# Second out projection tile for all tokens ahead of the third, and a re-ordered routing stage: weights copied aside, embedding products later, all rows on POOL, strips waited for one by one

## The reference, cut to what matters

```python
y = jax.nn.sigmoid(ma) * ya + jax.nn.sigmoid(mb) * yb
h = layer_norm_2(DEEPNORM_ALPHA * h + y @ w_out[i], ln1_g[i], ln1_b[i])
m = moe(h, w_router[i], b_router[i], w_up[i], b_up[i], w_down[i], b_down[i])
h = layer_norm_2(DEEPNORM_ALPHA * h + m, ln2_g[i], ln2_b[i])
h = h + jax.nn.sigmoid(h @ w_ple_gate[i] + b_ple_gate[i]) * (p[i] @ w_ple[i])
```

## Time and profile before

| | |
|---|---|
| median of 3 runs | 2378.13 us (2377.28 to 2379.11) |
| profiled execution, its own time | 2378.32 us |
| its span, first to last instruction | 2376.5 us |
| mean granted TensorE clock | 0.999 of full speed |
| busy | PE 98%, PEld 68%, DVE 50%, ACT 35%, POOL 8% |
| read from HBM | 663.69 MB, 280 GB/s over the span |

### The profile page before, as it was taken

How to read it: one execution, slowest core, us unless ns; L and a number is a source line. 1 busy time by engine, 2 the same in 40 slices (tenths; PEclk the granted TensorE clock), 3 DMA queues, 4 the chain that set the end, 5 groups by cost and what they waited for, 6 DMA issues and landing times.

```text
span 2376.5 us, 33062 instructions
## 1 busy us (share of the span) xinstructions
PE 2327.8 (98%) x13409; PEld 1604.4 (68%) x13409; DVE 1189.4 (50%) x1621; ACT 835.6 (35%) x1028; POOL 192.8 (8%) x90
## 2 busy tenths in 40 slices
PE   9999999999999999999999999999999999999999
PEld 8889989888888998988899983333333333333335
DVE  5668766756755876675686772112211111111115
ACT  4554344544544434454448341111111111111113
POOL 0002502200200250220020000000000000000000
PEclk9999999999999999999999999999999999999999
DMA  8765454565556545456546689999999999999995
GB/s 271 235 203 175 150 188 146 180 204 180 195 185 206 176 145 192 144 178 203 185 144 197 204 314 407 428 427 428 428 425 429 427 427 427 427 428 428 427 425 229
DMA packets 222323, 666.37 MB, mean 280 GB/s; under 512 B 10099, under 2 KB 164339, under 8 KB 191620
## 3 DMA queue, kind: packets, MB, share of 16 engines
q1 hardware_dynamic: 222212, 664.77, 73.6%
HBM read 663.69 MB, written 1.05 MB: 280 GB/s over the span
## 4 chain that ended last, share of the span: by engine, by line
PE 80%; DMA 15%; SPq 4%; DVE 0%; issue 0%; ACT 0%; ACTq 0%; POOLq 0%; DVEq 0%
PE ps L829 17%; PE ps L790 13%; DMA ring<-in_w_up_dram 13%; PE ps L811 12%; PE ps L1426 9%; PE ps L817 6%; PE ps L1474 6%; PE ps L916 4%; SPq L483 2%; DMA work<-in_w_down_dram 2%; PE ps L1391 1%; PE ps L1400 1%; PE ps L1006 1%; PE ps L1632 1%; PE ps L1266 1%; PE ps L1058 1%
## 5 line engine op out<-in xcount | busy, mean ns | idle before, releaser
L2305 DVE TENSOR_TENSOR ring_halves<-ring,ring_halves 128x2048 fp32r<-128x2048 f32 (+1 forms) x214 | 527.1, 2473 | 190.0 <-ACT ring_halves L1732 189.7
L1732 ACT CAST ring_halves<-ring 128x2048 fp32r<-128x2048 f32 (+1 forms) x214 | 401.4, 1876 | 114.9 <-PE ps L829 90.4
L2886 DVE TENSOR_TENSOR work<-ps,work 128x256 f32<-128x256 f32 x64 | 26.9, 420 | 633.3 <-PE ps L1460 633.3
L811 PE MATMUL ps<-x_halves,ring_halves 128*128 128x512 f32 x1280 | 326.5, 392 | 0.1
L1426 PE MATMUL ps<-ring,work 128*64 128x512 f32 x1248 | 278.1, 595 | 24.0 <-DMA ring<-in_w_up_dram 24.0
L829 PE MATMUL ps<-ring_halves,work_halves 128*128 128x512 f32 x1184 | 288.7, 391 | 0.3
L790 PE MATMUL ps<-x_halves,ring_halves 128*128 128x256 f32 x2208 | 274.7, 285 | 0.1
L790 PEld LDWEIGHTS ps<-x_halves,ring_halves 128*128 128x128 f32 x2208 | 267.6, 192 | 2.1 <-issue 0.7
L811 PEld LDWEIGHTS ps<-x_halves,ring_halves 128*128 128x128 f32 x1280 | 230.2, 189 | 41.5 <-issue 0.5
L829 PEld LDWEIGHTS ps<-ring_halves,work_halves 128*128 128x128 f32 x1184 | 221.4, 188 | 48.7 <-issue 3.1
L1720 ACT COPY hT<-ps 128x512 f32<-128x512 f32 x96 | 56.2, 585 | 497.5 <-PE ps L1426 460.5
(11 more groups left out here) (294 smaller groups left out, 2447.9 us busy)
## 6 DMA issues: line engine op xcount, KB each, us to landing
ring<-in_w_up_dram SPq DMA_DIRECT2D x77, 2048.0 KB, 36.5
work<-in_w_up_dram SPq DMA_DIRECT2D x37, 2048.0 KB, 41.6
ring<-in_w_down_dram SPq DMA_DIRECT2D x36, 2048.0 KB, 40.4
ring<-in_w_in_dram SPq DMA_DIRECT2D x52, 1024.0 KB, 5.2
ring<-in_ffn_up_dram SPq DMA_DIRECT2D x44, 1024.0 KB, 5.4
ring<-in_ffn_down_dram SPq DMA_DIRECT2D x44, 1024.0 KB, 4.9
ring<-in_ffn_gate_dram SPq DMA_DIRECT2D x43, 1024.0 KB, 5.4
work<-in_w_down_dram SPq DMA_DIRECT2D x19, 2048.0 KB, 36.6
```

The source lines that it names most:

```text
L811: return pe.matmul(ps[:, b, :], high[:, o:o + P], x_both[:, :, k, :], start=(k == 0), stop=(k == DT - 1))
L1732: nc.scalar.copy(second_half(high_of(name)[:], name), second_half(ring[:, s, :], name))\
L2305: v.tensor_tensor(second_half(ring_halves[s][:], name), second_half(ring[:, s, :], name), second_half(high_of(name)[:].bitcast(F32), name) ...
```

## The change

1. PE takes tile `w2o1` for both token tiles before `w2o2`. The transposes of t = 0 stand in the middle of the last tile of t = 1, behind its first half.
2. `router(t)` waits strip by strip, in the order 0, 4, 1, 5, 2, 6, 3, 7, where the even places are ACT's and the odd ones DVE's. The logits of t = 1 go to bank 1 (were in bank 2).
3. DVE's `best` is cut into `highest` (up to the cast) and `choose` (the marks). The order is: rows of t = 1, `highest(0)`, strips of t = 1, `choose(0)`, `highest(1)`, `choose(1)`.
4. POOL makes `h` of both token tiles; DVE's two instructions on rows (L2800, L2807) are gone. `h_ready` comes after POOL's fourth instruction.
5. ACT copies `w_ple` (128x2048) into `hn` once `h_ready` is there ("wple kept"). SP's loads into `V` and `IG` wait for that and for the fourth half product of t = 0.
6. The embedding products of t = 0 stand behind `router(1)` and around the counts; those of t = 1 are taken from the copy inside `few()`: one before `gate_up` of expert 0, three between it and the next gather. The gates' transpose moves into the branch too. ACT's copies and DVE's "rows in" move with them, DVE's into `step(HEAD)` after its selection.

```diff
-                    sp.wait_ge(dve_done.sem, dve_done.at("rows"))
-                    sp.wait_ge(pe_full.sem, pe_full.at(("ple", 1, 1)))
+                    sp.wait_ge(act_done.sem, act_done.at("wple kept"))
+                    sp.wait_ge(pe_full.sem, pe_full.at(("ple", 0, 1)))
...
-            for j in (1, 2):
-                y_part(j)
+            y_part(1)
+            for t in range(TT):
                 for kk in range(2):
-                    w2o_part(j, kk, 0)
+                    mm = w2o_part(1, kk, t)
+            release(mm, "w2o1")
+            y_part(2)
+            for kk in range(2):
+                w2o_part(2, kk, 0)
             y_part(3)
             full(w2o_last(0), ("t0", after))
-            for j in (1, 2):
-                for kk in range(2):
-                    mm = w2o_part(j, kk, 1)
-                release(mm, f"w2o{j}")
-            transposes(after, 0, hn)
-            release(w2o_last(1), "w2o3")
+            for kk in range(2):
+                mm = w2o_part(2, kk, 1)
+            release(mm, "w2o2")
+            release(w2o_last(1, lambda: transposes(after, 0, hn)), "w2o3")
...
-                for k in range(DT):
-                    mm = pe.matmul(ps[:, 2 * t, 0:32], hT[:, k, t * P:t * P + P], w(ROUTER + k * 32, 32),
+                for k in (0, 4, 1, 5, 2, 6, 3, 7):
+                    if k % 4 == 3:
+                        evacuated(t_bank(after, t) + k // 4, ("T", after, t))
+                    else:
+                        by = dve_done if k > 3 else act_done
+                        pe.wait_ge(by.sem, by.at(("turned", t, k)))
+                    mm = pe.matmul(ps[:, b, 0:32], hT[:, k, t * P:t * P + P], w(ROUTER + k * 32, 32),
                                    start=False, stop=(k == DT - 1))
...
             router(0)
             embedding(0, 0, 0)
             transposes(after, 1, hn)
+            router(1)
             embedding(0, 0, 1)
+            counts(0)
             embedding(0, 1, 0)
-            router(1)
+            counts(1)
             embedding(0, 1, 1)
-            counts(0)
-            embedding(1, 0, 0)
-            counts(1)
-            embedding(1, 0, 1)
...
+                    if ph == HEAD:
+                        for half, kk in ((0, 1), (1, 0), (1, 1)):
+                            embedding(1, half, kk, "few")
+                        for b in range(4, 8):
+                            emptied[b].add("rows in")
...
                 rows_turned("xg0", "xgt0")
+                gates_by_expert("few")
+                embedding(1, 0, 0, "few")
                 step(HEAD)
...
             pe.wait_ge(h_ready.sem, h_ready.at(("h", ("A",))))
-            pe.wait_ge(dve_done.sem, dve_done.at("rows"))
             pe.wait_ge(sel_ready.sem, sel_ready.at("sel0"))
             gather_rows("xg0")
-            embedding(1, 1, 0)
-            embedding(1, 1, 1)
-            open_bank(3, "gT")
-            pe.wait_ge(dve_done.sem, dve_done.at("gates"))
-            full(pe.transpose(ps[:, 3, 0:P], w(GATES4, P), ident[:]), "gT")
...
+            act.wait_ge(h_ready.sem, h_ready.at(("h", ("A",))))
+            done(nc.scalar.copy(wple_kept, w(V, 2 * D)), "wple kept")
...
-            def second_rows():
-                mine(("hn", ("A",), 1))
-                dve.wait_ge(lnp_in.sem, lnp_in.at((("A",), 1)))
-                done(v.tensor_tensor(h[:, 1, :], hn[:, 1, :], w(LNP["A"], D), ALU.mult), "scaled")
+            def first_highest():
                 dve.wait_ge(tables.sem, tables.at("all"))
-
-            ln(("A",), ("ln1_g_2", "ln1_b_2"), 0, ALPHA2, second_rows)
-            done(best(0), ("chosen", 0))
-            done(best(1), ("chosen", 1))
-            mine("scaled")
-            done(v.tensor_tensor(h[:, 1, :], h[:, 1, :], w(LNP["A"] + D, D), ALU.add), "rows")
+                highest(0)
+
+            ln(("A",), ("ln1_g_2", "ln1_b_2"), 0, ALPHA2, first_highest)
+            choose(0)
+            highest(1)
+            choose(1)
...
-                for t in range(1 if tag[0] == "A" else TT):
+                for t in range(TT):
                     pool.wait_ge(dve_done.sem, dve_done.at(("hn", tag, t)))
```

More of the change, by code:

```diff
@@ L1285, in _, with w2o_last @@
             release(mm, "w2o0")
-            def w2o_last(t):
+            def w2o_last(t, between=None):
                 for half in range(2):
@@ L1327, in _, with gates_by_expert @@
+            def gates_by_expert(branch):
+                open_bank(3, ("gT", branch))
+                pe.wait_ge(dve_done.sem, dve_done.at("gates"))
+                full(pe.transpose(ps[:, 3, 0:P], w(GATES4, P), ident[:]), ("gT", branch))
             pe.wait_ge(ple_in.sem, ple_in.at("wple"))
@@ L1544, in last_step @@
                     last_down((1, 2, 3))
-                for b in range(4, 8):
-                    emptied[b].add("rows in")
                 rows_turned("xg0", "xgt0")
+                gates_by_expert("few")
+                embedding(1, 0, 0, "few")
                 step(HEAD)
@@ L1594, in step @@
                     pe.wait_ge(dve_done.sem, dve_done.at((ph, "act", 3)))
+                gates_by_expert("many")
+                for half in range(2):
+                    for kk in range(2):
+                        embedding(1, half, kk, "many")
                 expert_biases()
@@ L1749, in evac_T @@
                                                bias=col(gname[1], i + k), scale=col(gname[0], i + k))
+                    if tag == ("A",) and k < 3:
+                        done(ins, ("turned", t, k))
                 ins.then_inc(emptied[b].sem, 1)
@@ L2168, in step @@
                     copy_out(1, gut[:, 512:1024])
+                    if ph == HEAD:
+                        for half in range(2):
+                            embedded(1, half, "few")
                     if ph != LAST:
@@ L2200, in many @@
                 act.sem_inc(emptied[2].sem, 1)
-                last_embedded()
+                embedded(0, 1)
+                gates_kept("many")
+                biases_kept("many")
+                for half in range(2):
+                    embedded(1, half, "many")
                 expert(HEAD)
@@ L2321, in evac_T @@
                                           col(gname[1], i + 4 + k), ALU.mult, ALU.add)
+                    if tag == ("A",) and k < 3:
+                        done(ins, ("turned", t, 4 + k))
                 ins.then_inc(emptied[b].sem, 1)
@@ L2857, in _ @@
             mine("gates")
-            act_event("bup")
             def biases_out():
@@ L2898, in step, with rows_into_banks @@
                              (ph, "acts", x))
-                mine("rows")
-                for t in range(TT):
-                    for half in range(2):
-                        b = 4 + 2 * t + half
-                        bank_empty(b, ("ple", 1 - t, half))
-                        ins = v.tensor_scalar(ps[:, b, :], h[:, t, half * 512:half * 512 + 512], ALPHA2, None, ALU.mult)
-                done(ins, "rows in")
+                def rows_into_banks():
+                    for t in (1, 0):
+                        for half in range(2):
+                            b = 4 + 2 * t + half
+                            bank_empty(b, ("ple", 0, half) if t else ("ple", 1, half, "few"))
+                            ins = v.tensor_scalar(ps[:, b, :], h[:, t, half * 512:half * 512 + 512], ALPHA2, None,
+                                                  ALU.mult)
+                    done(ins, "rows in")
                 step(HEAD, 0)
```

74 lines of the change are left out of this document (44 added, 30 removed).

## The result

The changed kernel took 2384.76 us (median of 8, 2382.96 to 2386.34) against 2377.86 for the kernel before beside it (median of 8, 2376.59 to 2379.25): +6.9 us, a ratio of 1.003 with an interval of 1.002 to 1.004. Forecast were +4 us and no change that can be measured; it is measurably slower. The profiled execution took 2385.56, its span 2383.8.

The account below looks back on a forecast made before the run. Weight loads bound the kernel; a late release of expert 1's first slots, 2.7 - 1.0 + 3.4 = 5.1 us, less 1.2 us of queue cushion gives +3.9, say +4: 2382.1 us, range 2378.0 to 2384.8.

Parts of the forecast that it names:

- What bounds the kernel: Expert weight loads set the pace at 425 to 429 GB/s; remaining bytes plus DMA idle time set the end.
- end = s less the cushion: At expert 1's first load the queue has 1.2 us to spare, the cushion; the end moves by s - 1.2.
- s: How much later expert 1's first slots are let go; forecast 2.7 - 1.0 + 3.4 = 5.1 us.
- The early load of slots 2 and 3 gives nothing: Loading from about 1404.3 instead of 1409.79 only moves the hole before 1416.20 behind it; no gain.
- The three products, +2.7: Three t = 1 embedding products between expert 0's `gate_up` and the next gather, unhidden, 0.91 us each: +2.7 us.
- From gather to `gate_up`, -1.0: The stretch from the gather to expert 0's `gate_up` shrinks from 5.1 to 4.1 us: -1.0.
- The shift of the gather, +3.4: DVE's waits for POOL make the choice 4.2 us later, a dropped sum gives back 0.8: gather +3.4 us.
- PEclk is 1.00 throughout: Expected sign in the profile: PE's granted clock stays at the full 2.4 GHz level throughout.
- the forecast case: Two DVE instructions in t = 1's choice wait for POOL, end +3.9, say +4 us; spans 2381.2 to 2383.2; 41%.
- the first rival: Only one DVE instruction, the cast, is shut out by POOL: gather +1.6, end +2.1 us, 2380.3; chance 24%.
- The term for the lock: DVE's SBUF to SBUF instructions, 128x1 and cast, wait for POOL's in t = 1's choice: 4.2 us later.
- the clock's rival: PE's clock falls to 1.2 GHz around the gather, costing another 1.9 us and more: 2384 to 2385.5; chance 18%.

Follow-up runs that it names:

- e4: Kernel before with six spare 512-column matmuls between `gate_up` of expert 0 and the next gather; 2382.78 us, +4.4 over the kernel before.
- e1: Changed kernel with nine small unused matmuls in PE's pauses around the transposes and router of t = 1; 2380.42 us, +2.0 over the kernel before.
- e12: The changed kernel run once more, unaltered, as the control on the last group's chip; 2384.10 us, +6.1 over the kernel before.
- e6: Kernel before with one spare 512-column matmul between `gate_up` of expert 0 and the next gather; 2378.61 us, +1.6 over the kernel before.
- e2: Changed kernel with `h` of t = 1 made by DVE again, POOL making only t = 0; 2384.42 us, +6.0 over the kernel before.
- e7: Kernel before with only the new order of out projection tiles and of t = 0's transposes; 2378.37 us, +1.4 over the kernel before.
- e8: Kernel before with strip-by-strip router, `highest`/`choose` split, t = 1 embedding products in PE's pauses, two behind the router's first strip; 2377.33 us, +0.3.
- e11: Kernel before with strip-by-strip router, `highest`/`choose` split, t = 1 embedding products moved forward, one behind the router's first strip; 2377.30 us, -0.7.
- e9: Changed kernel with nine spare small matmuls and the three embedding products behind `gate_up` cut to 32 of 512 columns; 2379.36 us, +1.4 over the kernel before.
- e10: Changed kernel with nine spare small matmuls and the kernel before's out projection order; 2378.80 us, +0.8 over the kernel before.
- e5: Changed kernel with nine spare small matmuls and `h` of t = 1 made by DVE; 2380.95 us, +3.9 over the kernel before.
- e3: Changed kernel with the three embedding products behind `gate_up` of expert 0 cut to 32 of 512 columns; 2383.15 us, +4.8 over the kernel before.

## Why the prediction was right or wrong

**What bounds the kernel: right.** The times follow the loads, within the limits told here. The DMA loss by 1480 us agrees with the time over the kernel before within 1.8 us for all thirteen (the changed kernel itself: 7.0 and 6.9), over a spread of 0 to 7 us, and behind it, from 1480 to 1680, all move 426 or 427 GB/s. Less than a microsecond or two it can't tell.

**The law "end = s less the cushion": right for a large s, not shown for a small one.** s was 7.3 with the offset out, by the law +6.1; measured were +6.9 and, in the control, +6.1. e4 bears it out without the rest of the change. The cushion itself is known to half a microsecond at best, since the landing on an empty queue varied from 7.7 (e1) to 8.8 (e12), and the one run made to show it, e6, came out at +1.6 in place of 0.

**The early load of slots 2 and 3 gives nothing: right.** The gap moved behind it. That a hole closed at 1433 would open again ahead of expert 1 shows in e1: between 1430 and 1440 it moved 412 GB/s, before 315; between 1440 and 1460 it moved 390, before 435.

**The three products, +2.7: about right.** From the start of `gate_up` of expert 0 to the next gather it is 16.7 us, before 13.8: +2.9. Taking them nearly out, which leaves 0.8 of them, moves s by 2.1 with the clock falling and by 2.0 with it held. In time: 1.6 and 0.6, with medians that are uncertain by about one.

**From gather to `gate_up`, -1.0: about right.** In the control, whose gather runs at full clock, it is 4.3 (1433.69 to 1438.02), and e1 has the same, where 4.1 was forecast and before shows 5.1: -0.8. In the trace of after it is 5.1 only because its gather still ran at half clock, 0.8 longer.

**The shift of the gather, +3.4: wrong.** It was +5.0 (in the control with the offset out, 5.05), and with -0.8, +2.9 and 0.1 behind the gather that makes the s of 7.3. The failed step is the sentence "PEclk is 1.00 throughout", on which the forecast case rested: it fell to 0.50 for ten us and made the products, the counts and the gather late. At full clock (e1) the gather came 1.7 us late, 1.2 with the offset out, near the first rival's figure (+1.6), not 3.4. So the clock added some 3.9 us ahead of the gather, for which the forecast case had nothing. The term for the lock was mis-sized in the same step: the 128x1 instruction was taken to be shut out like the 128x2 one, and it took 0.15. The Trainium skill, Vector Engine (DVE) Microarchitecture Reference, 5.1, had been read as including it; the trace does not bear that reading out. The Trainium skill, SBUF — State Buffer, "Who interferes with whom", agrees with this trace for the cast (1.73) and the mark (1.25).

**Why the clock was rated at 18%.** The argument against was that pauses of 0.7 us did nothing before and that the router's matmuls might bring the level back. The first looked at single pauses. The only fall that the prediction had seen it put behind "small matmuls and gaps"; the trace has few gaps there, since PE was busy for 7.84 of the eight us from 2338 to 2346, mostly with transposes and matmuls on one row. What the change did, as I read it, was take the cover away from several pauses together: in the kernel before, more products of 512 columns stand between the small matmuls, and the change moved them away to behind `router(1)` and into the branch. e1 shows the effect (nine small matmuls on constants hold the level), e2 that it comes without POOL, e7 that the old router with only a shifted start dips for some three us, and e8 and e11 that the products in the pauses hold it. But e7 leaves a rival: it has all the wide products of the kernel before and falls too, though not in every execution. No run has the changed routing with the old order of the out projection and without the spare matmuls, so what share the order has in the fall is open, and which of the pauses decides was not tried. Shown is that the nine spare matmuls hold the level and what that gives back.

**The account of 6.9 us.** Taken out one after the other, by s: 7.3 with all, 3.4 without the fall of the clock (e1: 3.9 us), 1.4 without the three products as well (e9: 2.0), and of the 1.4 that is left the cushion covers most. In medians the clock is 4.3 to 4.9 (e1 against the changed kernel, alone and each over its own before). The out projection's order, taken out of e1 alone, brings back 1.2 by s and 1.2 in the median (e10). Exchanging the wait for POOL for DVE's own rows brings back 0.2 by s and nothing in the median (e5). The clock is sure, and that the products come second; the small ones aren't sure to a microsecond.

**The range.** 2378.0 to 2384.8 holds the 2384.76 measured by 0.04 us, which is luck: the range reached so far only for the sake of the clock's rival, at 2384 to 2385.5. The forecast of "the same" failed because that rival had 18% and not the main part.

## What to carry to other kernels

A change that moves wide matmuls out of a stage of small ones can also take away what keeps PE's clock up: look at what the new order leaves PE to do between its pauses, and give the fall a term of its own, priced by the wide matmuls that follow (here 0.95 us for each product). Where the end is set by loads, the mean GB/s over a window that starts ahead of the stage and ends behind it gives the loss in one number, and it tells whether an earlier load closed a hole or only moved it. Two traces of one program can lie 0.7 us apart before the changed stage begins: take the offset at an event ahead of it, and subtract it, before a difference of that size is read as an effect. Work that looks hidden behind a backlog of PE is not hidden if PE's releases feed the queue with a cushion of only a microsecond or two.

## What the runs showed that I had not expected

**The last stage has a fall of the clock of its own, in some executions.** The executions of each kernel fall into two groups by their mean granted clock. For the kernel before: in the first group of chip runs 2377.32 us at 1.000 (15 executions) and 2379.08 at 0.999 (16), in the second 2376.92 (28) and 2378.41 (7), in the third 2377.24 (17) and 2379.03 (13). The difference is 1.5 to 1.8 us, as large as some of the effects that were looked for. The traces show one place. Windows of before there (the one of 2347 is the earlier trace rows), and under them those of the last stage in after and in e12_after_again, which are the same program (at the same time, though e12 is there some 0.8 us ahead):

```profile
2346.00:2347.00 1.00, 1.00 (x2) 0.54 (x3) 1.00 (x2) 0.72 (x1) 0.00 (x0) 0.60 0.79 320
...
2348.00:2349.00 1.00, 1.00 (x2) 0.34 (x1) 0.97 (x3) 0.91 (x1) 0.00 (x0) 0.50 0.03 12
```

```profile
2354.00:2355.00 1.00, 1.00 (x2) 0.34 (x1) 1.00 (x2) 1.00 (x2) 0.00 (x0) 0.50 0.40 164
```

```profile
2354.00:2355.00 1.00, 1.00 (x3) 0.40 (x3) 1.00 (x2) 0.90 (x2) 0.00 (x0) 1.00 0.07 29
```

In before and after, PE has half the clock there for some three us; in e12 the last stage runs at full clock. So the same program falls there or doesn't. By the executions at 1.000 alone, each over the kernel before at 1.000 of its group, e1 is at +3.1 (2380.42, 3 executions), e5 at +3.0 (2379.93, 4), e4 at +5.5 (2382.78, 7), e6 at +1.6 (2378.56, 9), e7 at +1.2 (2378.10, 6), e9 at +1.2 (2378.46, 3), e10 at +1.3 (2378.56, 9), e8 at +0.2 (2377.15, 8) and e11 at -0.5 (2376.77, 7): e5 is then no longer slower than e1, and e4 and e6 are 1.2 and 1.6 us later than the law with its cushion gives. One trace at 0.999 (e11) shows no fall at this place, but one some 25 us ahead of it, in the last expert. A window of it:

```profile
2322.00:2323.00 1.00, 1.00 (x6) 0.42 (x4) 0.93 (x4) 0.00 (x0) 0.00 (x0) 0.50 1.00 418
```

The traces of e2, e3 and e12 have it too, between 2325 and 2331, beside the fall in the routing. What it costs wasn't measured.

**POOL doesn't shut out every small instruction.** Beside POOL's two-input instructions the cast on 128x8 (1.73), the mark on 128x32 (1.25) and the one on 128x2 (1.65) were held until POOL's ended. The one on 128x1 (0.15), the search for the eight highest (0.20) and for their places (0.18), and the strips that are read from PSUM were not. Whether the shape or the kind of instruction decides can't be told from these.
